# Attention units in pairs of heads on halves of the array, and the compression's first products on column halves

## What is computed

```python
# group C (NSA): 8 heads in 2 kv groups (g), head = 4 g + j; here seq = 256, so all blocks are
# selected and the window holds all keys: both branches are causal attention, with their own k and v
def compress(a, pos, w1, w2):                    # 32 positions x 64, stride 16
    return jax.nn.gelu(blk @ w1) @ w2            # w1: 2048 x 64, w2: 64 x 64
k_cmp = compress(k_c, pos_k, k_w1, k_w2)
v_cmp = compress(v_c, pos_v, v_w1, v_w2)
p_c = masked_softmax(qb @ k_cmp * scale)         # o_c = p_c @ v_cmp
p_s = masked_softmax(qrb @ ks * scale)           # o_s = p_s @ vs
p_w = masked_softmax(qrb @ kw * scale)           # o_w = p_w @ vw
o = gb[..., 0:1] * o_c + gb[..., 1:2] * o_s + gb[..., 2:3] * o_w
# group A (DSA): 4 heads; an indexer keeps the top 64 keys of each query
score = relu(iq @ ik * IDX_DIM ** -0.5) @ iw ; _, sel = lax.top_k(score, 64)
a_out = softmax over sel of (q . k) * scale, times v
# group B (S5): a complex diagonal scan, then y = gelu(y); y = y * sigmoid(y @ glu_w + glu_b)
x = x + concat(rms_norm(a_out), rms_norm(b_out), rms_norm(c_out)) @ w_out
x = x + square(relu(rms_norm(x) @ w_up)) @ w_down
```

## Time and profile before

| | us |
|---|---|
| median of 3 runs (731.89 to 733.95) | 733.24 |
| the profiled execution's own time | 735.1 |
| its span | 733.1 |
| busy: PE, PE's weight loads | 664.8, 586.9 |
| busy: DVE, ACT, POOL | 450.8, 367.1, 228.2 |

### The profile page before, as it was taken

One profiled execution on the slowest core, in us unless ns is written; L12 is line 12 of the kernel. 1 busy time (PEld: TensorE's weight loads), 2 busy tenths in 40 slices (PEclk: granted clock), 3 DMA queues, 4 the chain that ended last, 5 costly groups with the idle time before them and its releaser, 6 DMA issues.

```text
span 733.1 us, 11482 instructions
## 1 busy us (share of the span) xinstructions
PE 664.8 (91%) x4308; PEld 586.9 (80%) x4308; DVE 450.8 (61%) x860; ACT 367.1 (50%) x680; POOL 228.2 (31%) x379
## 2 busy tenths in 40 slices
PE   5959878779899999999999987977989999999996
PEld 4847767568798899988978886756879889999884
DVE  8675974843755559596555659584375555455553
ACT  5542755563544543445545567556354444444542
POOL 5899433441034399980000001544100000000001
PEclk9988998998999999999999999999899999999998
DMA  9485020200685555637535722020065665666541
GB/s 267 125 220 149 30 41 30 73 30 29 202 237 201 170 186 169 225 119 247 168 119 164 228 79 41 30 73 30 29 202 178 196 188 171 208 182 198 177 140 57
DMA packets 62965, 102.77 MB, mean 140 GB/s; under 512 B 20677, under 2 KB 27022, under 8 KB 62878
## 3 DMA queue, kind: packets, MB, share of 16 engines
q1 hardware_dynamic: 58862, 98.63, 44.1%
q0 software_dynamic: 592, 1.70, 0.9%
q10 hardware_dynamic: 3456, 1.70, 0.9%
HBM read 99.66 MB, written 1.31 MB: 138 GB/s over the span
## 4 chain that ended last, share of the span: by engine, by line
PE 72%; DVE 14%; ACT 6%; issue 3%; DMA 2%; POOL 1%; SPq 0%; DVEq 0%; POOLq 0%; ACTq 0%
PE pb L1542 70%; DVE w_lo L1179 5%; DMA raw<-in_w_in 2%; DVE tab_zone L1437 2%; DVE x L1109 1%; ACT w_hi L804 1%; DVE dtmp L1102 1%; ACT tab_zone L1000 1%; PE pb L1675 1%; DVE h_lo L1109 1%; ACT ptmp L1007 1%; DVE cprob L1102 1%; PE pb L1825 1%; POOL sp L584 1%; ACT tab_zone L998 1%
## 5 line engine op out<-in xcount | busy, mean ns | idle before, releaser
L1179 DVE TENSOR_TENSOR w_lo<-raw,w_hi 128x1024 fp32r<-128x1024 f32 (+2 forms) x176 | 225.3, 1298 | 157.3 <-ACT w_hi L804 157.2
L804 ACT ACTIVATE w_hi<-raw 128x1024 fp32r<-128x1024 f32 (+2 forms) x184 | 187.7, 1026 | 224.4 <-PE pb L1542 200.4
L1542 PE MATMUL pb<-h_hi,w_hi 128*128 128x256 f32 x512 | 145.2, 284 | 2.5 <-DVE h_lo L1109 1.8
L1542 PE MATMUL pb<-h_hi,w_lo 128*128 128x256 f32 x512 | 144.9, 283 | 0.0
L1542 PE MATMUL pb<-h_lo,w_hi 128*128 128x256 f32 x512 | 144.9, 283 | 0.0
L1542 PEld LDWEIGHTS pb<-h_hi,w_hi 128*128 128x128 f32 x512 | 98.2, 192 | 4.1 <-DVE w_lo L1179 3.0
L1542 PE MATMUL pb<-w_hi,z_hi 128*128 128x512 f32 x256 | 99.9, 390 | 0.4 <-DVE w_lo L1179 0.4
L1542 PE MATMUL pb<-w_hi,z_lo 128*128 128x512 f32 x256 | 99.8, 390 | 0.0
L1542 PE MATMUL pb<-w_lo,z_hi 128*128 128x512 f32 x256 | 99.6, 389 | 0.0
L1542 PEld LDWEIGHTS pb<-h_hi,w_lo 128*128 128x128 f32 x512 | 98.2, 192 | 0.4
L1542 PE MATMUL pb<-w_hi,h_hi 128*128 128x512 f32 (+2 forms) x224 | 85.8, 383 | 13.9 <-DVE w_lo L1179 10.8
(11 more groups left out here) (304 smaller groups left out, 982.4 us busy)
## 6 DMA issues: line engine op xcount, KB each, us to landing
raw<-in_w_up SPq DMA_DIRECT2D x64, 512.0 KB, 3.7
raw<-in_w_down SPq DMA_DIRECT2D x64, 512.0 KB, 4.3
raw<-in_w_in SPq DMA_DIRECT2D x24, 512.0 KB, 4.7
raw<-in_w_out SPq DMA_DIRECT2D x16, 512.0 KB, 3.8
raw<-in_w_in SPq DMA_DIRECT2D x8, 308.0 KB, 3.5
raw<-in_w_in SPq DMA_DIRECT2D x8, 280.0 KB, 3.3
x<-in_x ACTq DMA_DIRECT2D x4, 256.0 KB, 4.2
u_zone<-proj SPq DMA_DIRECT2D x16, 32.0 KB, 2.1
```

Source lines behind the costliest of these rows:

```text
L804: hi_made.by(act.activation(w_hi[:, n % RING, 0:width(n)], raw[:, n % RING, 0:width(n)], ACT.Copy))
L1179: lo_made.by(dve.tensor_tensor(w_lo[:, n % RING, 0:width(n)], raw[:, n % RING, 0:width(n)], w_hi[:, n % RING, 0:width(n)].bitcast(F32), AL ...
L1542: return pe.matmul(o, l, r, start=start, stop=stop, skip_group_check=True)
```

## The change

The 20 units become 10 *pairs*: heads j and j+4 of group C for one branch (8 pairs), or two heads of group A (2 pairs). The two heads of a pair lie on partitions 0 to 63 and 64 to 127 of q and k. Their scores are four matmuls, two on each half of the array's rows, into `pb[0]` and `pb[1]`; their products with the values are four matmuls, two on each half of the columns, and read `proj` and `av` directly, so `vpad` and all zero halves go. The two score banks belong to one pair, so PE waits for DVE's maxima of a pair before it starts the next one; `ex`, `sc`, `pn` and `pT` hold two pairs (`sc` in a tile of its own). Pair p's scores, pair p-2's transposes and pair p-3's product follow one another. Each engine does a pair's work in one go; DVE makes one reciprocal and one gate product for it. `c_first` interleaves keys and values on the two column halves, so that the gelu lies on 128 partitions by 32 columns; `w2` and `w2d` are spread likewise. The cone and gate products of `c_probs` are merged. `kT`, `akT` and `av` are written in one operation where two were. As group C's heads are now stored in the order (j, g), `gain_c` and the rows of `w_out` are loaded in that order, with two DMAs where one was (`TWO_LOADS`). The clearings of `av`, `vpad`, `gk` and `gvr` go, one of `w2` comes. The tables of side work are written anew.

Cut to its core:

```diff
+TWO_LOADS = (P_IN + 1, P_IN + 2, P_IN + 4, P_IN + 5)
...
+def landed(n):
+    return 16 * sum(2 if i in TWO_LOADS else 1 for i in range(n % RING, n + 1, RING))
...
+        pairs = [("C", br, b) for b in range(4) for br in range(2)] + [("A", 0, b) for b in range(2)]
...
@@ SP, output pieces
-                        piece(n, raw[:, n % RING, :].rearrange("p (k n) -> p k n", k=2),
-                              wo_l[:, 2 * q:2 * q + 2, half * 512:half * 512 + 512])
+                        if q < 2:
+                            piece(n, dst, wo_l[:, 2 * q:2 * q + 2, half * 512:half * 512 + 512])
+                        else:
+                            for g in range(C_KV):
+                                piece(n, dst[HD * g:HD * g + HD], wo_c[:, g, 2 * q - 4:2 * q - 2, half * 512:half * 512 + 512])
...
@@ POOL
-                    if u >= 3:
-                        pool.wait_ge(pT_ps.sem, pT_ps.at(L, u - 2))
...
-                    if u in (3, 7, 11, 15):
-                        lo_out(20 + u // 4)
+                    if p >= 2:
+                        pool.wait_ge(pT_ps.sem, pT_ps.at(L, p - 1))
+                    for m in range(2):
+                        i = 2 * (p % 2) + m
+                        for t, (a, b) in enumerate(((0, PART), (PART, 384))):
+                            w = pool.tensor_tensor(pn[:, i, a:b], ex[:, i, a:b],
+                                                   cf[:, i, t:t + 1].to_broadcast([PART, b - a]), ALU.mult)
...
+                    if p in (1, 3, 5, 7):
+                        lo_out(20 + p // 2)
...
@@ ACT
-                            m = act.activation(dst, src[:].rearrange("p (b n) -> p b n", b=2), ACT.Copy,
-                                               scale=mhalf[:, g:g + 1])
+                        m = act.activation(kT.rearrange("p b t -> p (b t)"), src[:], ACT.Copy)
...
-                for br, o in ((0, O_VS), (1, O_VW)):
-                    step(act.activation(vpad[:, :, br, :, 64:128],
...
+                    if p in (1, 2):
+                        transposed(6 + p - 1)
+                    if p in (1, 2, 4, 6):
+                        hi(L, 20 + (1, 2, 4, 6).index(p))
...
@@ DVE
-                    for t in (av, vpad):
-                        step(dve.memset(t[:], 0.0), False)
...
-                    step(dve.tensor_copy(gt[:, 0, :], pb[4][0:HD, 0:64]))
+                    step(dve.tensor_copy(gt[:, 0, :], pb[4][:, 0:32]))
...
-                between = {0: (top8_of_rest,), 1: (top8_of_rest,), 2: (c_open1,), 3: (top8_of_rest,),
-                           4: (c_gelu,), 5: (top8_of_rest,), 6: (top8_of_rest,), 7: (y_cube, c_keys),
-                           9: (y_gelu, c_max, top8_of_rest), 10: (top8_of_rest,), 11: (top8_of_rest,),
-                           12: (c_probs,), 13: (a_mask,), 15: (y_half,), 17: (y_glu,),
+                between = {0: (top, top), 1: (c_open1, top), 2: (c_gelu, top), 3: (top, y_cube, c_keys),
+                           4: (top, y_gelu), 5: (c_max, top), 6: (c_probs, top), 7: (a_mask, y_half), 8: (y_glu,),
...
+                        dve.wait_ge(s_ps.sem, s_ps.at(L, p + 1))
+                        if p >= 2:
+                            dve.wait_ge(e_sb.sem, e_sb.at(L, p - 1))
...
@@ PE
-                    for kv in range(2):
-                        for q in range(16):
-                            m = mm(pb[4][0:HD, kv * 32:kv * 32 + 32], w1[:, kv, q, :],
-                                   cx[:, kv, q].rearrange("p g n -> p (g n)"), (kv, q) == (0, 0), q == 15)
+                    for q in range(16):
+                        for kv in range(2):
+                            m = mm(pb[4][HD * kv:HD * kv + HD, 0:32], w1[:, kv, q, :],
+                                   cx[:, kv, q].rearrange("p g n -> p (g n)"), q == 0, q == 15)
...
+                between = {0: (c_first, a_keys), 1: (a_queries,), 2: (c_second, s5_out), 4: (c_scores,),
+                           6: (y_turned,), 7: (c_transpose, glu), 8: (c_values,)}
+                for p in range(UNITS + 3):
+                    if p < UNITS:
+                        kind, br, b = pairs[p]
+                        if p >= 1:
+                            pe.wait_ge(s_sb.sem, s_sb.at(L, p))
+                        q, k = (cqrT[:, b], kT[:, br]) if kind == "C" else (aqT[:, b], akT[:, b])
+                        for t, (a, n) in enumerate(((0, PART), (PART, SEQ))):
+                            for m in range(2):
+                                d = slice(HD * m, HD * m + HD)
+                                w = mm(pb[m][:, a:a + n], q[d, t * PART:(t + 1) * PART], k[d, 0:n], t == 0, True)
+                        s_ps.by(w)
+                    if 2 <= p < UNITS + 2:
+                        v = p - 2
+                        pe.wait_ge(pn_sb.sem, pn_sb.at(L, v + 1))
+                        if v >= 1:
+                            pe.wait_ge(pT_sb.sem, pT_sb.at(L, v))
...
+                        for t in range(TT):
+                            for m in range(2):
+                                w = mm(o[HD * m:HD * m + HD, t * PART:SEQ], vs[t][m],
+                                       pT[:, 2 * (v % 2) + m, t * SEQ:SEQ + t * PART],
+                                       t == 0 and v in (0, C_PAIRS // 2, C_PAIRS), t == 1 and last)
```

More of the change, by code:

```diff
@@ L298, in trunk @@
         vec_ps, vec_sb = sig("vec_ps", 0), sig("vec_sb", 0)
-        raw_in = [sig(f"raw_in{i}", 16 * PIECES // RING) for i in range(RING)]
+        raw_in = [sig(f"raw_in{i}", landed(PIECES - RING + i)) for i in range(RING)]
         hi_made = sig("hi_made", PIECES)
@@ L402, in trunk @@
         p_steps = ctx.enter_context(nc.semaphore("p_steps"))
[L404 to L410, removed]
+        pairs = [("C", br, b) for b in range(4) for br in range(2)] + [("A", 0, b) for b in range(2)]
+        C_PAIRS = C_HEADS
         def load_b(eng, lyr, s):
@@ new lines, in _ @@
+                top = top8_of_rest
+                between = {0: (top, top), 1: (c_open1, top), 2: (c_gelu, top), 3: (top, y_cube, c_keys),
+                           4: (top, y_gelu), 5: (c_max, top), 6: (c_probs, top), 7: (a_mask, y_half), 8: (y_glu,),
+                           9: (lambda: h_rest(8, gm[:, L], out_rows, K_ORDER, 0, 4),),
+                           10: (lambda: h_rest(8, gm[:, L], out_rows, K_ORDER, 4, 2),)}
+                assert sum(w.count(top) for w in between.values()) * 8 == TOPK
@@ L1840, in _ @@
-                        mm(o, vs[0], pT[:, u % 2, 0:SEQ], u in (0, C_HEADS, 2 * C_HEADS), False)
-                        pv_done.by(mm(o[:, PART:SEQ], vs[1], pT[:, u % 2, SEQ:384], False,
-                                      (kind == "A" or b > 2) and h % 2 == 1 and br == (kind == "C")))
-                    for work in between.get(i, ()):
+                            vs = [[av[:, t, 2 * b + m, :] for m in range(2)] for t in range(TT)]
+                        last = (kind == "A" or b > 2) and br == (kind == "C")
@@ L1844, in _ @@
+                        for t in range(TT):
+                            for m in range(2):
+                                w = mm(o[HD * m:HD * m + HD, t * PART:SEQ], vs[t][m],
+                                       pT[:, 2 * (v % 2) + m, t * SEQ:SEQ + t * PART],
+                                       t == 0 and v in (0, C_PAIRS // 2, C_PAIRS), t == 1 and last)
+                        pv_done.by(w)
+                    for work in between.get(p, ()):
                         work()
```

265 lines of the change are left out of this document (119 added, 146 removed).

## The result

The changed kernel takes 742.78 us (median of 9 runs, 739.77 to 745.38), the kernel before, in runs beside them, 733.95 (9 runs): ratio 1.0108, 95% interval 1.0080 to 1.0136. It is slower by 8 us by the ratio (8.8 by the two medians), where 732.5, a gain of 0.7, was forecast.

The account below looks back on a forecast made before the run. PE bounds the full stretches; the attention phases are a loop between engines, DVE's place mattering most. Layer 1 +1.0, layer 0 −1.0, switches +0.6, start −1.3 make −0.7 on 733.24: 732.5 us, range 727 to 738.

Parts of the forecast that it names:

- The hidden work: Attention phases: pairing saves PE about 15 us per layer, nearly all hidden; c_first's 1.9 us is covered by DVE's list.
- changes of mode: Switches between row halves, whole array and column halves: sixty at 0.1 us, three per layer on the path, +0.6 in all.
- Row halves: A pair's scores on PE: 0.65 us with full overlap, taken, or 1.3 us with none.
- rival 3: Row halves don't overlap: 0.65 us at each of some five scores on the path, +3.2, 735.7 us; chance 0.10.
- Rival 5: Tiling switches drain on the path, thirty of sixty at 0.1 us: +3.0, 734.9 us, or 738 at 0.2 each; chance 0.05.
- The layout: Layer 1's attention phase laid out by durations: gains 2.5 at s5_out, 2.1 at c_probs, −1.3 at its end if clock stays high.
- The clock: Emptier PE makes low-clock stretches likelier: +1.5 s5_out, +1.5 glu, +1.6 tail; middles taken, layer 1 +1.0, layer 0 −1.0.
- rival 2: Longer PE gaps bring the lower clock ahead of s5_out, glu and tail: +3.4, 736.6 us; chance 0.19.
- the upper end: Layer 0's phase at worst: +0.8, named as 1.5 kept, tail 1.6 more, less 1.3 and 1.0 of slack behind s5_out.
- The start: Start of layer 0: without DVE's clearings of av and vpad, POOL's early products and first tile's scale come sooner, −1.3 us.
- Rival 6: Start of layer 0: the clearings held nothing on POOL, so no gain there: 733.8 us; chance 0.06.
- The range: Whole kernel: 727 to 738 us, leaving out only what lies beyond the forecast's rivals.

Follow-up runs that it names:

- a_fill: Changed kernel plus 86 extra unused matmuls per layer on PE ahead of the waits where it stood idle: 728.65 us, ratio 0.9898 to the kernel before.
- b_fill: Kernel before plus 42 extra unused matmuls per layer ahead of PE's waits: 724.90 us, ratio 0.9863 to the kernel before.
- The experiment with serial order: a_fill with scores, value products and c_first doing one array half first, then the other, instead of alternating: 729.89 us, ratio 0.9950.
- b_clear: Kernel before with the clearings of av and vpad moved from ahead of the fifth weight piece's low part to the twelfth's: 733.67 us, ratio 0.9971.
- a_tail: Changed kernel plus extra matmuls only ahead of the last two pairs' transposes, 17 and 14 per layer: 737.36 us, ratio 1.0044.
- a_fine_fill: Changed kernel with handoffs by head instead of by pair, plus a_fill's extra matmuls and somewhat more: 723.24 us, ratio 0.9852.
- a_order: a_fine_fill with group B's output transposes after pair 7's product instead of pair 6's, and nine extra matmuls removed: 718.46 us, ratio 0.9779.
- a_spread: Changed kernel plus 60 extra matmuls per layer spread behind the pairs' scores and products, not in the long waits: 735.24 us, ratio 1.0018.

## Why the prediction was wrong

**The hidden work: right, and less of it than forecast.** Of a_fill's extra matmuls 81 lie in the window (its 584 records are 162 more than 422), and of b_fill's all 42. With these taken off at 0.26 us each, PE works 36.2 us (57.3 − 81 x 0.26) with pairs and 48.4 (59.3 − 42 x 0.26) without: 12 us less, where 14 to 15 were forecast, and the phase is no shorter. The shortfall is that a pair's round costs more than half of two units' (see the changes of mode). c_first takes 2.17 us in the changed kernel and 2.06 at the high level, as forecast. The first maximum of layer 1 is set by DVE. The experiment with serial order gives the share of c_first's cost that shows: half in layer 1.

**Row halves: right in the main.** A pair's scores take 0.86 us, not 0.65 and not 1.3; rival 3 falls.

**Changes of mode: under-sized.** A round of a pair is 0.86 + 0.80 + 0.81 = 2.47 us; without switches it would be 0.65 + 0.66 + 0.65 = 1.96, from the spacings in the earlier trace rows (a unit's transposes are 0.33). Put down to three switches, the difference is 0.17 each instead of 0.1; but 0.65 for scores and products supposes halves that overlap wholly, which no run shows, and the transposes, which use the whole array, alone exceed theirs by 0.14. If all sixty were on the path, that would be 10 us. They were not: at equal clock a phase with pairs is 0.7 us longer in all, with this and the coarser handoffs in it. Rival 5 is thus no more than a part. By the Trainium skill's rule of the drain ("TensorEngine Tiling (Array Packing)", Key Properties) each switch costs something. The 0.14 to 0.17 is in line with it. The pairs still spend 0.8 us less per round than two units (2.47 and 3.26).

**The layout: right at the high clock, and the comparison made with it wrong.** Forecast were 15.8, 38.7 and 65.5 us from the first maximum to the ends of s5_out, c_probs and the phase; a_fill shows 16.4, 37.0 and 64.7. But I set these times of a kernel at full clock against a kernel before whose own phase held 10 us at the lower level. At equal clock that one takes 64.0: where I wrote −1.3, it is +0.7. One term was too dear: c_probs took 4.2 us before (484.41 to 488.60), I took 0.5 off that, and it takes 2.5 (487.65 to 490.10). I had left POOL's piece beside its large product; the piece now starts behind it, at 489.86, and the product is 0.57 long instead of 2.47. The tail eats this: forecast 26.8 us (486.5 to 513.3), in a_fill 27.7.

**The clock: the step that failed.** Mechanism and sign were right, and with them rival 2: "longer gaps bring the lower clock". The term was mis-sized: for layer 1 I added 1.5, 1.5 and 1.6 at three places, each time a single short block, and then took the middle of an interval, so that 2.3 of these 4.6 us entered the sum. Measured are 4.8 (70.2 less 65.4). In the changed kernel the clock over the phase is 0.73, so it was at 1.2 GHz for 38 of 70 us (2 x 0.27 x 70.2), where before it was 11 of 67.5 (2 x 0.08 x 67.5, at a cost of 2.8 us). That 4.8 is near 4.6 is luck in part: of the three places s5_out's last records lost 0.7 (2.56 us to the next scores, 1.86 in a_fill), the glu nothing (1.92 in both) and the tail 1.7, while 2.3 fell ahead of s5_out, where I had put nothing.

For layer 0 the working has a slip: the terms that it names for the upper end come to −0.7 (1.6 − 1.3 − 1.0), and +0.8 only with the glu's 1.5 in it. The phase measured +0.8 in the traces, where −1.0 was forecast, though b_clear's trace shows that a repeat can move a phase by 2 us. I also put at nothing, without a reason, what happens outside the phases: the low stretch that begins in the tail runs on into the sums and the first output tile, 2.3 us in layer 0. So layer 1 came to +2.7 for +1.0, layer 0 to +0.8 for −1.0, and the stretch behind it to +2.3 for nothing: 5.8 us, against the 5.6 between the forecast's −0.7 and the trace's +4.9. (The 0.6 for switches is within the phases, and some 0.4 lie in the full stretches.)

**The start: right.** Forecast −1.3; the first maximum of layer 0 comes 1.4 sooner, with the clearings moved alone 1.1. Rival 6 falls: without the clearing two of POOL's products take 0.88 or 1.01 us, with it 2.18. I had said near 0.5: a w_lo of DVE's still runs beside them. The Trainium skill, "SBUF — State Buffer", Who interferes with whom, would have a DVE instruction without a second SBUF input, outside the 2-port modes, leave GpSimd alone on this chip; here the measurement decides otherwise for this clearing.

**The range.** Its upper end, 738, took in rival 2 at +3.4 and nothing beyond. 736.6 was that rival's time; the measured 742.8 is 6 above: 2.3 of that is the stretch behind layer 0's phase, which no rival held. The two traces show 4.9 us of the loss; some 4 us between the medians lie beyond them and stay open.

## What to carry to other kernels

In a phase where PE isn't the bound, count its idle time as a cost: work taken off PE there may come back as a lower clock, in the phase and at the start of the full stretch behind it. Compare two layouts at the same granted clock (look at the clock column of the stretch first), else the clock of one is booked as a gain of the other. Where PE has waits of some microseconds ahead of work on the path, unused matmuls in them were worth 1 to 2% here, in either kernel, and only then did finer handoffs show their full size (2.7 us of a phase against 1.3). One trace of each kernel is thin ground for differences below 2 us in a phase.

## What was not expected

In the phases of the kernel before, a low stretch lasted 3.4 us, as this one:

```profile
114.20:117.60 3.40, 3.40 (x75) 3.40 (x68) 0.00 (x0) 0.00 (x0) 0.00 (x0) 0.50 0.02 5
```

After the change several last 10 us, as from 475 to 485, with PE busy all along: work on the path did not bring the clock back at once. The longest, over layer 0's tail, the sums and the first output tile, lasts 20 us (154.5 to 174.5).

A low stretch can also come in one run and not in another, at the same place of the order. In the traces of b_fill, a_tail, a_fine_fill, a_order and a_spread one lies between 190 and 204 us, in the full work behind layer 0's phase; from the first output matmul to layer 1's first maximum these five take 280.2 to 282.2 us, the other seven, which lack it, 277.4 to 279.4. PE's busy time from 185 to 205 is the same, 17.86 us, in b_fill, at a clock of 0.91, and in the kernel before, at 1.00. It may be part of what spreads the times of one kernel; that was not tested.

And c_first's 32-column halves ran at once only when they alternated (2.06 against 3.71 us), while for the scores and products, 128 and 256 columns wide, the order made no difference (0.86 and 0.80 or 0.81 us). Whether that is the width is not shown: the serial c_first has 32 matmuls of one half in a row, the scores and products two.
